# A hybrid decoder layer in fp32 on one core: the last part of the output projection in quarters, 2 MB down weights, a scatter of its own for expert 30, another order of the first loads

## What is computed

```python
h = h + jnp.concatenate([out_a, out_b], axis=-1) @ w_out          # output projection
u2 = _rmsnorm(h, g_ffn)
logits = u2 @ w_router + b_router
top_val, top_idx = lax.top_k(logits, TOP_K)                        # 4 of 32
gates = jax.nn.softmax(top_val, axis=-1)
...
gu = xb @ w_gu[e] + b_gu[e]                                        # [rows,1024] @ [1024,2048]
gate = jnp.minimum(gu[:, :D_FF], SWIGLU_LIMIT)
lin = jnp.clip(gu[:, D_FF:], -SWIGLU_LIMIT, SWIGLU_LIMIT)
act = (lin + 1.0) * gate * jax.nn.sigmoid(SWIGLU_ALPHA * gate)
return act @ w_down[e] + b_down[e]                                 # [rows,1024] @ [1024,1024]
...
y_prompt = _rmsnorm(hp[:, N_META:], g_final)
```

## Time and profile before

| | |
|---|---|
| median of 3 runs | 1103.86 us (1103.79 to 1105.02) |
| profiled execution: its time / its span | 1106.28 us / 1104.2 us |
| mean granted TensorE clock | 0.987 |
| busy: PE, DVE, ACT, POOL | 1070.4 us (97%), 345.5 (31%), 191.2 (17%), 15.0 (1%) |
| moved by DMA | 425.84 MB, mean 386 GB/s |
| expert stage, `gu` / `dn` on PE | 463.3 us / 228.6 us |

### The profile page before, as it was taken

How to read it: one execution, slowest core, us unless ns; L and a number is a source line. 1 busy time by engine, 2 the same in 40 slices (tenths; PEclk the granted TensorE clock), 3 DMA queues, 4 the chain that set the end, 5 groups by cost and what they waited for, 6 DMA issues and landing times.

```text
span 1104.2 us, 13367 instructions
## 1 busy us (share of the span) xinstructions
PE 1070.4 (97%) x5237; PEld 442.2 (40%) x5237; DVE 345.5 (31%) x649; ACT 191.2 (17%) x311; POOL 15.0 (1%) x39
## 2 busy tenths in 40 slices
PE   7999999999999999999999799999999999999995
PEld 5758553333333333333333233333333333333331
DVE  5854331122222222222222222222222222222242
ACT  3463321111111111111111011111111111111111
POOL 3100000000000000000000000000000000000000
PEclk9999999999999999999999899999999999999997
DMA  9651697999999999999999999999999999999992
GB/s 316 238 189 50 265 378 298 424 425 425 424 427 425 424 424 426 426 427 426 425 425 424 424 423 426 426 426 425 424 424 426 426 426 426 426 426 426 424 417 93
DMA packets 54146, 425.84 MB, mean 386 GB/s; under 512 B 7407, under 2 KB 14182, under 8 KB 21322
## 3 DMA queue, kind: packets, MB, share of 16 engines
q1 hardware_dynamic: 53416, 424.67, 92.6%
q0 software_dynamic: 512, 0.26, 0.1%
q10 hardware_dynamic: 162, 0.09, 0.0%
HBM read 422.69 MB, written 2.35 MB: 385 GB/s over the span
## 4 chain that ended last, share of the span: by engine, by line
PE 76%; DMA 22%; issue 1%; DVE 1%; SPq 0%; ACT 0%; DVEq 0%
PE ps L1448 31%; DMA mem<-in_w_gu 19%; PE ps L1464 15%; PE ps L1474 6%; PE ps L1171 6%; PE ps L1423 6%; PE ps L1329 3%; DMA mem<-in_w_down 2%; PE ps L1499 2%; PE ps L1430 2%; PE ps L1217 1%; DMA mem<-in_w_in 1%; PE ps L1492 1%; PE ps L1353 0%; PE ps L1388 0%
## 5 line engine op out<-in xcount | busy, mean ns | idle before, releaser
L1448 PE MATMUL ps<-mem 128*64 128x512 f32 x2048 | 463.3, 600 | 12.2 <-DMA mem<-in_w_gu 6.5
L1448 PEld LDWEIGHTS ps<-mem 128*64 128x64 f32 x2048 | 141.9, 138 | 300.5 <-issue 282.1
L1464 PE MATMUL ps<-mem 128*64 128x512 f32 x1024 | 228.6, 599 | 3.8 <-DMA mem<-in_w_down 3.8
L1071 DVE TENSOR_TENSOR mem<-ps,bguT 128x512 f32<-128x512 f32 x64 | 41.2, 686 | 372.2 <-PE ps L1499 372.2
L1097 DVE TENSOR_TENSOR yacc<-ps,yacc 128x1024 f32<-128x1024 f32 x93 | 108.3, 1217 | 140.7 <-PE ps L1474 140.7
L1464 PEld LDWEIGHTS ps<-mem 128*64 128x64 f32 x1024 | 74.0, 138 | 150.9 <-issue 147.6
L1474 PE MATMUL ps<-mem 64*128 64x512 f32 x384 | 91.3, 607 | 0.0
L685 ACT ACTIVATE mem<-ps 128x512 f32<-128x512 f32 x32 | 19.1, 597 | 399.8 <-PE ps L1423 397.7
L1423 PE MATMUL ps<-mem 128*64 128x512 f32 x372 | 85.1, 592 | 0.0
L1171 PE MATMUL ps<-mem 128*128 128x280 f32 x256 | 64.4, 410 | 2.0 <-DMA mem<-in_w_in 2.0
L1058 DVE TENSOR_TENSOR mem<-slot_no,pos 128x192 f32<-128x192 f32 x32 | 11.5, 359 | 153.1 <-PE ps L1423 152.8
(11 more groups left out here) (298 smaller groups left out, 475.0 us busy)
## 6 DMA issues: line engine op xcount, KB each, us to landing
mem<-in_w_gu SPq DMA_DIRECT2D x128, 2048.0 KB, 23.9
mem<-in_w_down SPq DMA_DIRECT2D x128, 1024.0 KB, 25.4
mem<-in_w_in SPq DMA_DIRECT2D x5, 2048.0 KB, 17.8
mem<-in_w_out SPq DMA_DIRECT2D x1, 4096.0 KB, 13.9
mem<-in_state_gla SPq DMA_DIRECT2D x8, 128.0 KB, 2.4
mem<-v_rows SPq DMA_DIRECT2D x4, 256.0 KB, 5.2
out_gla_s<-mem SPq DMA_DIRECT2D x8, 128.0 KB
yacc<-in_x_prompt SPq DMA_DIRECT2D x1, 512.0 KB, 5.2
```

The lines of the kernel that those rows point to most:

```text
L1071: dve.tensor_tensor(hS[:, n, :].rearrange("p (k s) -> p k s", k=8), turned[:, n], bguT[:, 8 * n:8 * n + 8, bass.ds(e_of(i - 1), 1)].broadc ...
L1448: last = pe.matmul(ps[S * w:S * w + S, n, :], xT[:, k % 4, k // 4, :], weights[:, col:col + 512], start=(k == 0), stop=(k == KD - 1))
L1464: last = pe.matmul(ps[S * w:S * w + S, bank, :], acts[:, k, :], weights[:, col:col + 512], start=(k == 0), stop=(k == KD - 1))
```

## The change

Four parts. (1) **First loads**: `wxa` is issued ahead of `wlr`, and POOL waits for the first `uT` before it starts its sixteen loads. (2) **Last half in quarters**: the second half of chunk 1 is done as two quarters of 256 columns, `(1, 1)` and `(1, 2)`; transposes and rank matmuls and six of eight router steps of chunk 1 stand between the first quarter and the end of the second; `u2` of chunk 1 is now made in two steps, a product with the gains on DVE (`gained`) and the scale on ACT; `turn_bgu(0)` is moved ahead and `turn_bgu(1)` behind the last `first_rows`. `out_done` must now reach 6 for the held-back loads. (3) **Down weights** in two pieces of 2 MB: four rows of `w_down` to a partition, so a descriptor of 16 KB; `turn_gu` and `turn_bgu` read every fourth column instead of every second. The four loads of expert 31 stay at 1 MB. (4) **Expert 30** gets its own scatter ahead of expert 31's down projection, and DVE three more `collect`.

```diff
@@ @block.sync
+            load(wxa, win[:, :, 0:512], "in_xa")
             load(wlr[:, :, 0:GR], win[:, :, 2560:2576], "in_lr")
-            load(wxa, win[:, :, 0:512], "in_xa")
...
-                src = A["w_down"][0, bass.ds(e_of(i), 1), r:r + 2 * P, :].rearrange("e (p k) n -> p (e k) n", p=P)
-                load(half_of(e, p).rearrange("p (k n) -> p k n", k=2), src, f"piece_in{p}")
+                src = A["w_down"][0, bass.ds(e_of(i), 1), r:r + 4 * P, :].rearrange("e (p k) n -> p (e k) n", p=P)
+                load(down_of(e, p).rearrange("p (k n) -> p k n", k=4), src, f"piece_in{p}")
...
-            sp.wait_ge(sem("out_done"), 5)
+            sp.wait_ge(sem("out_done"), len(nth_half))
             gate_linear(GU[3], 1, 1)
             down(DN[0], 0, 0)
-            down(DN[1], 0, 0)
             sp.wait_ge(sem("used0"), 1)
             down(DN[2], 0, 0)
-            down(DN[3], 0, 0)
@@ @block.gpsimd
             pool.wait_ge(sem("x1_in"), 16)
+            pool.wait_ge(sem("uT_ready"), 1)
@@ @block.scalar
             evacuate(1, 1, 7)
+            square(1, 2)
+            evacuate(1, 2, 4)
             act.wait_ge(sem("var_h"), 2)
             root(1)
+            act.wait_ge(sem("rstd_last"), 2)
+            act.activation(u2[:, 1, :], u2[:, 1, :], ACT.Copy, scale=rstd[:, 1:2]).then_inc(sem("u2_ready"), 1)
@@ @block.vector
+            def gained(k0, k1):
+                cols = slice(k0 * P, k1 * P)
+                return dve.tensor_tensor(u2[:, 1, cols], yacc[:, 1, cols], gff[:, cols], ALU.mult)
...
             choose(2, 0)
+            add_h(1, 1)
+            dve.wait_ge(sem("h_ready"), nth_half[1, 1])
+            link(gained(0, 6))
             choose(0, 1)
...
-            add_h(1, 1)
-            variance(1)
-            normalised(1)
+            add_h(1, 2)
+            dve.wait_ge(sem("h_ready"), nth_half[1, 2])
+            gained(6, 8).then_inc(sem("rstd_last"), 1)
...
+                for c in range(TC):
+                    dve.wait_ge(sem("scattered"), TC * n + c + 1)
+                    collect(c)
@@ @block.tensor
-                    last = pe.transpose(ps[:, 2 + f // 4, (f % 4) * P:(f % 4 + 1) * P], guS[:, 2 * P * (f // 2) + f % 2:2 * P * (f // 2 + 1):2], ident[:, :])
+                    last = pe.transpose(ps[:, 2 + f // 4, (f % 4) * P:(f % 4 + 1) * P], guS[:, 4 * P * (f // 4) + f % 4:4 * P * (f // 4 + 1):4], ident[:, :])
...
                 turn_weights(n, 6)
+                pe.wait_ge(sem("yS_ready"), n)
+                pe.wait_ge(sem("GT_ready"), n)
+                pe.wait_ge(sem("biased"), 2 * n + 2)
+                spread_rows(GT, yS, True, True)
                 pe.wait_ge(sem("act_ready"), n + 1)
...
-                pe.wait_ge(sem("yS_ready"), n)
-                pe.wait_ge(sem("GT_ready"), n)
-                pe.wait_ge(sem("biased"), 2 * n + 2)
-                spread_rows(GT, yS, True, False)
+                pe.wait_ge(sem("added"), TC * n)
                 pe.wait_ge(sem("yS_ready"), n + 1)
                 pe.wait_ge(sem("GT_ready"), n + 1)
-                spread_rows(GT_end, yS_end, False, True)
+                spread_rows(GT_end, yS_end, True, True)
```

More of the change, by code:

```diff
@@ L377, in down_ahead @@
             def down_ahead(i, e):
-                for p in DN:
+                for p in DOWN:
                     landed(p, i - 1)
@@ L985, in add_h @@
                 dve.wait_ge(sem("out_done"), nth_half[c, n])
[L986 to L992, removed]
+                k0, k1 = PARTS[c, n]
+                dst = yacc[:, c, k0 * P:k1 * P]
+                dve.tensor_tensor(dst, ps[:, OUT_BANK[c, n], 0:(k1 - k0) * P], dst, ALU.add).then_inc(sem("h_ready"), 1)
+            def gained(k0, k1):
+                cols = slice(k0 * P, k1 * P)
+                return dve.tensor_tensor(u2[:, 1, cols], yacc[:, 1, cols], gff[:, cols], ALU.mult)
             def normalised(c):
@@ L1022, in _ @@
             add_h(0, 1)
-            variance(0)
+            dve.wait_ge(sem("sq_h"), nth_half[0, 1])
+            dve.tensor_tensor(ssq[:, 0:1], halves[:, 0, 0:1], halves[:, 1, 0:1], ALU.add).then_inc(sem("var_h"), 1)
             normalised(0)
@@ L1026, in _ @@
             choose(2, 0)
+            add_h(1, 1)
+            dve.wait_ge(sem("h_ready"), nth_half[1, 1])
+            link(gained(0, 6))
             choose(0, 1)
+            dve.wait_ge(sem("sq_h"), nth_half[1, 1])
+            link(dve.tensor_tensor(ssq[:, 1:2], halves[:, 0, 1:2], halves[:, 1, 1:2], ALU.add))
             dve.wait_ge(sem("rank_done"), 1)
@@ L1344, in turn_h @@
                 pe.wait_ge(sem("h_ready"), nth_half[c, q])
-                for k in range(4):
-                    last = pe.transpose(ps[:, bank, k * P:(k + 1) * P], yacc[:, c, (4 * q + k) * P:(4 * q + k + 1) * P], ident[:, :])
+                k0, k1 = PARTS[c, q]
+                for k in range(k0, k1):
+                    last = pe.transpose(ps[:, bank, (k - k0) * P:(k - k0 + 1) * P], yacc[:, c, k * P:(k + 1) * P], ident[:, :])
                 last.then_inc(sem("h_turned"), 1)
@@ L1374, in _ @@
             turn_h(1, 0, 4)
-            project_out(1, 1, range(MA, KD - 2))
+            project_out(1, 2, range(4))
+            turn_h(1, 1, 7)
             pe.wait_ge(sem("tri_ready"), 1)
@@ L1381, in _ @@
             pe.matmul(ps[:, 0, 2 * NE:3 * NE], tri, mk[:, 0, :], start=False, stop=True).then_inc(sem("rank_done"), 1)
-            project_out(1, 1, range(KD - 2, KD))
-            pe.matmul(ps[:, 1, 0:NE], ones[0:TL, :], mk[0:TL, 2, :], start=True, stop=False)
-            pe.matmul(ps[:, 1, 0:NE], ones[:, :], mk[:, 0, :], start=False, stop=False)
+            pe.wait_ge(sem("hT_ready"), nth_half[1, 1])
+            logits(1, 6, range(6))
+            project_out(1, 2, range(4, KD))
             def first_rows(c, start, stop):
@@ L1389, in first_rows, with turn_bgu @@
                 return last
+            def turn_bgu(half):
+                rows = slice(32 + 32 * half, 64 + 32 * half)
+                for f in range(8):
+                    last = pe.transpose(ps[:, 3, NE * (8 * half + f):NE * (8 * half + f + 1)], spread[rows, 4 * P * (f // 4) + f % 4:4 * P * (f // 4 + 1):4], ident[rows, rows])
+                last.then_inc(sem("bgu_turned"), 1)
+            pe.wait_ge(sem("bgr_in"), 32)
+            turn_bgu(0)
+            turn_h(1, 2, 4)
+            pe.matmul(ps[:, 1, 0:NE], ones[0:TL, :], mk[0:TL, 2, :], start=True, stop=False)
+            pe.matmul(ps[:, 1, 0:NE], ones[:, :], mk[:, 0, :], start=False, stop=False)
+            pe.wait_ge(sem("hT_ready"), nth_half[1, 2])
+            logits(1, 6, range(6, KD)).then_inc(sem("lg_done"), 1)
             pe.wait_ge(sem("sel_first"), 1)
@@ L1393, in _ @@
             first_rows(2, True, False)
[L1394 to L1405, removed]
-            pe.wait_ge(sem("hT_ready"), nth_half[1, 1])
-            logits(1, 6, range(4, KD)).then_inc(sem("lg_done"), 1)
-            pe.wait_ge(sem("bgr_in"), 32)
-            turn_bgu(0)
             pe.wait_ge(sem("mask_ready"), 3)
             pe.matmul(ps[:, 1, 0:NE], tri, mk[:, 1, :], start=False, stop=True).then_inc(sem("rank_done"), 1)
-            pe.wait_ge(sem("bgu_turned"), 1)
-            turn_bgu(1)
+            first_rows(0, False, False)
             pe.wait_ge(sem("sel_ready"), 1)
@@ L1416, in _ @@
             first_rows(1, False, True).then_inc(sem("gathered"), 1)
+            pe.wait_ge(sem("bgu_turned"), 1)
+            turn_bgu(1)
             def gather(n):
```

47 lines of the change are left out of this document (29 added, 18 removed).

## The result

The changed kernel takes **1092.82 us** (median of 4 runs, 1092.21 to 1093.78) beside 1104.07 us before on the same chip: ratio 0.990, 95% interval 0.988 to 0.9915, so 11.2 us or 1.0% faster. Two later groups of five rounds gave 0.9887 (0.9871 to 0.9902) and 0.9889 (0.9872 to 0.9906), 12.8 and 12.3 us by their medians. The profiled execution took 1092.21 us, with a span of 1090.7; it is the quickest of its four, while the profiled one of before (1106.28, span 1104.2) was slower than all of its four, so the two traces are 13.5 us apart in span where the medians are 11.2 apart.

What follows compares the result with a forecast made beforehand. End is set by when DMA runs without pause, bytes over rate, and what follows the last landing. Gains 1.0 + 3.4 + 3.6 + 3.7 = 11.7 us, so 1103.86 - 11.7 = 1092.2 us; range 1087 to 1099.

Steps and rivals of the forecast that it cites:

- held-back loads: Rival at the DMA start: they come later than `used0`, so DMA starts no sooner; under 1 us, inside the forecast.
- Part 1, 1.0 us: Program start: `wxa` lands sooner, so PE projects at 13.5 instead of 14.50; gain 1.0 us, bounds 0 and 1.1.
- they take about 0.6 us: First loads: the 64 KB in 64-byte pieces ahead of `wxa` were said to take about 0.6 us.
- Part 2, 3.4 us: Projection to first gate matmuls: `used0` moves 3.4 us sooner, 0.65 + 4.3 - 1.5; bounds 0.65 and 4.9.
- The layout by hand: Router stage: new order laid out with earlier durations, gate matmuls starting at 163.85 instead of 166.62.
- I take 1.5 us as still lost: Router stage: of up to 4.3 us lost to half clock, 1.5 us would remain lost because narrow work still stands together.
- Part 3, 3.6 us: Expert stream: 426 instead of 421 GB/s from 16 KB descriptors, 0.115 us x 31 experts; gain 3.6 us, bounds 0 and 5.
- Part 4, 3.7 us: Program end: first chunk complete 16.8 us after expert 30's last landing instead of 20.5; gain 3.7 us, bounds 1.9 and 3.7.
- the layout behind the landing: Program end: scatter to 7.5 us, down halves to 11.0 and 15.1, ACT's copy to 15.8, first chunk at 16.8.
- The stride: Rival in the expert stage: transposes with every fourth column make PE the bound; 1101.7 or 1116.9 us, chance 0.10.
- The rate was real: Its rival, in the expert stream: the rate does not come from the descriptor, so no gain there; 1095.8 us, chance 0.10.
- the clock did not fall in the router stage: Its rival: clock falls again or ACT's `u2` scale is late, bringing only 0.65 us; 1094.9 us, chance 0.12.

Runs made afterwards that it cites:

- The kernel with chunk 2 joint: Against the changed kernel, expert 30's scatter of chunk 2 moved behind expert 31's down projection: 1092.05 us, and 1092.41 beside 1093.24 in one group.

## Why the prediction was right

Forecast 1092.2, measured 1092.8; the four terms added to 11.7, the medians fell by 11.2 to 12.8. What bounds the kernel was right, and so was what each part acts on, but for part 1. That the sum fits so closely is partly luck: a term that was too small and two that were too large cancel.

- **What bounds it.** The moment when DMA runs on, the rate, and what follows the last landing account for all 13.5 us between the two spans, and in the table above the middle term follows the size of the runs alone. The held-back loads, late by 0.2 us, cost nothing.
- **Part 1, 1.0 us: wrong.** The step that failed is "they take about 0.6 us", read from one low stretch at 6 to 7 us and put down to the 64-byte pieces. The dip stays without them, the 2 MB take as long, and 0.4 us of earlier issue is all: the projection starts at 14.08, not at 13.5. The medians show 0.2 and -0.15.
- **Part 2, 3.4 us: too small.** Undoing it costs 4.3 us in one group, 4.8 across two and 3.7 in the traces; from before to after it is 5.3, since the kernel before lost its clock earlier. The layout by hand was right: from the first `turn_h` of chunk 1 to the gate matmuls it has 21.7 us (142.17 to 163.85) at full clock, and 21.6 were seen. The step that failed is "I take 1.5 us as still lost": in eleven profiles of the new order nothing was lost. With that term at nothing the sum has 4.9.
- **Part 3, 3.6 us: right in mechanism and size.** 3.4 and 4.2 by the two kernels without 16 KB descriptors, 4 by the traces. That the size came out of one stretch of 5 us and one of 13 is luck in part: in the same trace, stretches of 5 us between 700 and 765 move anything from 410 to 444 GB/s, and those with gate pieces alone 423 to 433. By the three cycles of the Trainium skill (DMA: Bandwidth & Descriptors, Why small descriptors are slow) the estimate was 1.7 us; the measurement is twice that and decides.
- **Part 4, 3.7 us: too large.** 3.0 from landing to first chunk in the traces of before and after, 2.2 (1.9 in the traces) by the run without it. The clock rose as said and ACT's bare copy was foreseen to the digit (0.74 against 0.75). The step that failed is the layout behind the landing, 16.8 us where 17.5 were seen. ACT's two copies end at 4.9 us as laid out, but the scatter starts 0.25 later and takes 2.85 instead of 2.7, each half of the down projection 3.65 instead of 3.5, and the second half starts at 11.9, not 11.5. The rest of the way down to 1.9 is not the scatter's: the coarser loads had already shortened the pause.
- Undone one at a time the parts cost 0.2, 4.3, 3.4 and 2.2 us, 10.1 in all, of 12.3 to 12.8 in the same groups. Most of the missing 2 us and more is parts 3 and 4 at the end of the program. Alone on the end of before (20.4 us from landing to first chunk), coarser loads take off 1.1 (19.3) and a scatter apart takes off 3.8 (16.7), but both together only 3.0 (17.5). So either part, taken away from the whole, looks 1.9 us cheaper than it is alone. What is left is within the spread of such sums.

**The rivals.** The stride did not make PE the bound: 2 ns more per weight load, so 0.5 us in all even if it were bare. The rule of the Trainium skill (SBUF — State Buffer, Door 1) that the prediction used, two hits to a 16-byte line, would have had a price here between every second and every fourth fp32 column; the trace shows none for these weight loads (207 and 209 ns), and it shows one between every column and every second (146 to 207) that the rule would not give. The same passage also calls four fp32 columns the stride that is free; the 61 ns at every second column do not fit that either. The rate was real, the clock did not fall in the router stage in any profile of the new order, and the held-back loads never ruled. The worst case of the prediction, 1100.3, lies outside its own range (to 1099); the result is far from both.

## What to carry to other kernels

When one stream of loads never pauses, list three prices only: when it starts, its rate, what stands behind its last landing. Work on an engine beside it cost nothing here; a matmul ahead of its first freed buffer or behind its last landing did. The order of narrow matmuls and waits just ahead of such a point can cost more through TensorE's clock than by its length, as it did here (2.8 us of 3.7), so look at the granted clock in 5 us stretches; putting wide matmuls that must be done anyway between the narrow ones is worth a try, and went with full clock in all eleven profiles here. A low rate in one short stretch names no culprit: see whether it goes away with the transfer. And measure a rate difference of half a percent over the whole stream, from a fixed issue to a fixed landing, not over 5 us. Last, two parts that shorten the same pause do not add up: undoing each one alone shows too little of both.

## What the runs showed of the hardware

- **Descriptor size above 8 KB still counts.** 8 KB runs to a partition give 425 GB/s over 700 us with two loads or four to an expert, 16 KB runs 427; over the stream that is about 4 us (900.4 to 900.8 us against 896.1 to 896.7).
- **The order of steps moves the clock.** Half clock in three profiles of one order and in none of eleven of the other: 3.7 us in the traces and 4.3 to 4.8 by the medians, of which the reordering saves about 0.85 us at equal clock.
- **Early in the run PE is slow for a varying time.** The same sixteen records of the low-rank product behind the first projections took 1.08 us in two executions of the whole change and 1.49 in a third; in the kernel before they took 1.99:

```profile
18.60 1.99 PE ps L1183 x16
```
```profile
18.11 1.08 PE ps L1207 x16
```

  The eight projection records ahead of them take 4.10 us, where sixteen of the same take 3.97 later (at 74.10 in the chain of before). The clock column reads 1.00 from 13 to 22 us in all these traces, so it doesn't show this slowness; whether it is the clock stays open.

  The kernel with chunk 2 joint, which does the same up to there, took 2.03 in one execution and started its gate matmuls 0.8 us later than the changed kernel. That is a spread of about a microsecond, as between runs of one kernel, and it hides a gain like that of part 1.
